# Third layer of a four-layer model: the recurrence woven, pair by pair, between units of its own later projections

## The reference, cut to what matters

```python
def hgrn2_mixer(h, w_in, lb, gate_norm_w, w_out):
    proj = h @ w_in
    q, f, i, g = jnp.split(proj, [HGRN_FDIM, 2 * HGRN_FDIM, 2 * HGRN_FDIM + D_MODEL], axis=-1)
    q = jax.nn.silu(q)
    log_f = jnp.logaddexp(jnp.log(lb), jnp.log1p(-lb) + jax.nn.log_sigmoid(f32))
    k = (1.0 - lb) * jax.nn.sigmoid(-f32)
    o = hgrn2_recurrence(q.reshape(shp), k.reshape(shp), log_f.reshape(shp), i.reshape(...))
    o = rms_norm(o, gate_norm_w) * jax.nn.silu(g.reshape(...))
    return o.reshape(B, S, D_MODEL).astype(h.dtype) @ w_out
```

## Time and profile before

| | |
|---|---|
| median of 3 runs | 2283.85 us (2283.8 to 2285.46) |
| profiled execution | 2282.78 us |
| its span, first to last instruction | 2280.8 us |
| PE busy, share of the span | 2151.5 us, 94% |
| VectorE busy | 1072.6 us, 47% |
| ScalarE busy | 823.5 us, 36% |
| GpSimd busy | 225.3 us, 10% |
| mean granted clock of PE | 0.963 |

### The profile page before, as it was taken

How to read it: one execution, slowest core, us unless ns; L and a number is a source line. 1 busy time by engine, 2 the same in 40 slices (tenths; PEclk the granted TensorE clock), 3 DMA queues, 4 the chain that set the end, 5 groups by cost and what they waited for, 6 DMA issues and landing times. The chain is left out here.

```text
span 2280.8 us, 27066 instructions
## 1 busy us (share of the span) xinstructions
PE 2151.5 (94%) x10717; PEld 1772.2 (78%) x10717; DVE 1072.6 (47%) x1877; ACT 823.5 (36%) x1515; POOL 225.3 (10%) x347
## 2 busy tenths in 40 slices
PE   6999989999999999999897999999899979999998
PEld 5887557888887877878786888888778658888887
DVE  5343766565554345233984533433433555334333
ACT  3154754443333234322012422323432664223322
POOL 8200000100000001001542100000100011000000
PEclk9999999999999999999656999999999989999999
DMA  5435412233332222322000223322233103222321
GB/s 127 99 111 92 52 38 88 82 99 99 104 93 93 93 93 82 103 101 74 1 1 9 94 93 100 103 93 93 84 129 129 56 1 102 93 93 96 107 93 74
DMA packets 162107, 192.00 MB, mean 84 GB/s; under 512 B 22866, under 2 KB 133757, under 8 KB 161981
## 3 DMA queue, kind: packets, MB, share of 16 engines
q1 hardware_dynamic: 157536, 176.15, 24.4%
q0 software_dynamic: 3904, 13.97, 3.3%
q10 hardware_dynamic: 541, 0.15, 0.0%
HBM read 182.91 MB, written 7.34 MB: 83 GB/s over the span
## 5 line engine op out<-in xcount | busy, mean ns | idle before, releaser
L1396 DVE TENSOR_TENSOR WHL<-raw,WHL 128x1024 fp32r<-128x1024 f32 x312 | 385.6, 1237 | 700.3 <-ACT WHL L869 700.0
L869 ACT ACTIVATE WHL<-raw 128x1024 fp32r<-128x1024 f32 x312 | 328.5, 1054 | 570.3 <-PE bank L2247 395.6
L2247 PE MATMUL bank<-WHL,HXh 128*128 128x512 f32 x1632 | 442.7, 393 | 5.4 <-DVE HXl L1405 4.0
L2098 PE MATMUL bank<-HXh,WHL 128*128 128x512 f32 x1120 | 438.8, 392 | 4.1 <-ACT BIG L1026 1.6
L2100 PE MATMUL bank<-HXh,WHL 128*128 128x512 f32 x1120 | 436.6, 390 | 0.0
L2247 PEld LDWEIGHTS bank<-WHL,HXh 128*128 128x128 f32 x1632 | 308.4, 190 | 72.4 <-issue 7.2
L2099 PE MATMUL bank<-HXl,WHL 128*128 128x512 f32 x928 | 361.6, 390 | 0.0
L2247 PE MATMUL bank<-WHL,HXl 128*128 128x512 f32 x816 | 252.9, 391 | 0.0
L2098 PEld LDWEIGHTS bank<-HXh,WHL 128*128 128x128 f32 x1120 | 211.0, 188 | 49.4 <-issue 5.4
L2100 PEld LDWEIGHTS bank<-HXh,WHL 128*128 128x128 f32 x1120 | 210.7, 188 | 44.3
L2099 PEld LDWEIGHTS bank<-HXl,WHL 128*128 128x128 f32 x928 | 174.5, 188 | 35.5
(11 more groups left out here) (322 smaller groups left out, 3052.4 us busy)
## 6 DMA issues: line engine op xcount, KB each, us to landing
raw<-in_mlp_w_up_dram SPq DMA_DIRECT2D x64, 512.0 KB, 4.6
raw<-in_mlp_w_down_dram SPq DMA_DIRECT2D x64, 512.0 KB, 4.3
raw<-in_w_up_dram SPq DMA_DIRECT2D x44, 512.0 KB, 5.1
raw<-in_a_w_in_dram SPq DMA_DIRECT2D x32, 512.0 KB, 4.5
raw<-in_w_in_dram SPq DMA_DIRECT2D x24, 512.0 KB, 4.8
raw<-in_w_down_dram SPq DMA_DIRECT2D x22, 512.0 KB, 4.3
raw<-in_w_kv_dram SPq DMA_DIRECT2D x16, 512.0 KB, 4.5
rel_dram<-GB POOLq DMA_DIRECT2D x1, 5120.0 KB, 54.0
```

The source lines that it names most:

```text
L869: return a.activation(dst, src, ACT.Copy, **k)
L1396: v.tensor_tensor(dst(1), src, dst(0).bitcast(F32), ALU.subtract).then_inc(w_lo, 1)
L2098: m.matmul(b[:, :], w[0][:, k, :], x[0][:, k, :], start=(k == 0), stop=False)
L2247: ins = m.matmul(ybank(tt, h)[:, :], x, w[:, h * HALF:(h + 1) * HALF], start=(k == 0 and i == 0), stop=(k == nk - 1 and i == 2))
```

## The change

The weights of this layer are cut into eight blocks and used in a new order: qf0 (query and forget projections of heads 0 and 1), hi0, qf1, hg0, qf2, hi1, qf3, hg1, where hi and hg blocks are halves of 512 columns. qf0 is done in `norm_halves(3)`. The recurrence starts then: pair p has 8 steps, and step s holds the level product of the pair and, behind it in PE's stream, dense unit 8p + s, as long as there is one (28 in all; in the first step of a pair the level product stands in the middle of the unit). The level products of a pair share two banks (5 and 7), the dense units have four (4, 6, 0, 2), and states, keys, outputs and turns of the pair before use banks 1 and 3. VectorE and GpSimd treat a pair in one operation of twice the columns. The full decay is multiplied into hQ and hK in place, and the chunk states go into used parts of hF. The output product is cut by column half and feature block (`out_product`, 12 products): two pieces stand in steps 5 and 6 of the last pair, four between the last two heads' work, and ten follow. Its weights are loaded as blocks of 512 columns. The arithmetic is the same. The core of the diff (left out: renamed counters and most of the lines that the new loops replace, the bodies of the products, the masked copy of a pair, the per-head helpers that lose an argument, the new helpers of ScalarE, `projected`, `dense_out`, `out_high`, `keys_evac`, which evacuate one dense unit, then split the unit three ahead, round a feature block of the output, or copy the turned keys):

```diff
+DENSE = ("hi0", "qf1", "hg0", "qf2", "hi1", "qf3", "hg1")
...
+    for name in ("qf0",) + DENSE:
+        i = int(name[2:])
+        if name[:2] == "qf":
+            cols8(name, a_in, 256 * i, 256)
+            cols8(name, a_in, D + 256 * i, 256, at=1)
+        else:
+            blocks(name, a_in[:, (2 if name[:2] == "hi" else 3) * D:][:, 0:D], i)
+    blocks4("h_out", t["a_w_out_2"][0])
...
-          ("hq", 8, "act"), ("hf", 8, "act"), ("hi", 8, "vec"), ("hg", 8, "act"),
+          ("qf0", 4, "act"), ("hi0", 4, "vec"), ("qf1", 4, "act"), ("hg0", 4, "act"), ("qf2", 4, "act"),
+          ("hi1", 4, "vec"), ("qf3", 4, "act"), ("hg1", 4, "act"),
...
+        def state(h, c):
+            return hF[:, h, (384, 0, 128)[c]:(384, 0, 128)[c] + P]
+        def of_pair(x, p):
+            return x[:, 2 * p:2 * p + 2, :].rearrange("p h t -> p (h t)")
+        LV, DB = (bank[5], bank[7]), (bank[4], bank[6], bank[0], bank[2])
...
+            for p in range(HH // 2):
+                a, b = 2 * p - 2, 2 * p - 1
+                for l in range(1, NL):
+                    w = LEVELS[l]
+                    pool.wait_ge(s_grown, NL * p + l)
+                    pool.wait_ge(lv_psum, level_count(p, l if l > 1 else 0))
+                    g.tensor_tensor(halves_of(klv, w)[0], halves_of(of_pair(hK, p), w)[0], halves_of(sfx2, w)[0],
+                                    ALU.mult).then_inc(klv_ready, 1)
+                    if l == 4 and p:
+                        head_gain(a)
+                        head_gain(b)
+                        head_stats(a)
+                if p:
+                    head_stats(b)
+                pool.wait_ge(s_grown, NL * (p + 1))
+                g.tensor_tensor(of_pair(hK, p), of_pair(hK, p), sfx2, ALU.mult).then_inc(ks_ready, 1)
+                if p < HH // 2 - 1:
+                    pool.wait_ge(ks_ready, p + 1)
+                    g.memset(sfx2, 1.0).then_inc(s_set, 1)
...
+            for p in range(HH // 2):
+                a_, b_ = 2 * p - 2, 2 * p - 1
+                for s in range(NL + 1):
+                    if p and s == 1:
+                        if p > 1:
+                            head_evac(b_ - 2)
+                        keys_evac(a_)
+                    elif p and s == 2:
+                        keys_evac(b_)
+                    elif p and s == 4:
+                        head_out(a_)
+                    elif p and s == 6:
+                        head_evac(a_)
+                        head_out(b_)
+                    if 8 * p + s < 4 * len(DENSE):
+                        dense_out(8 * p + s)
+                    if p == HH // 2 - 1 and s == 3:
+                        for k in range(4):
+                            out_high(k)
+            w, a_, b_ = unit_at["h_out", 0], HH - 2, HH - 1
+            out_high(4)
+            split(w + 3)
+            head_evac(5)
+            keys_evac(a_)
+            out_high(5)
+            keys_evac(b_)
+            split(w + 4)
+            head_out(a_)
+            head_out(b_)
+            split(w + 5)
+            head_evac(a_)
+            out_high(6)
+            head_evac(b_)
+            out_high(7)
+            split(w + 7)
+            split(unit_at["up0", 0] + 1)
...
+            def level_ops(p, l):
+                w = LEVELS[l]
+                ends = [2 * T // (2 * w), w]
+                f1, f2 = halves_of(of_pair(hF, p), w)
+                if l:
+                    vec.wait_ge(lv_psum, level_count(p, l))
+                    vec.wait_ge(vec_chain, grown[0])
...
                 else:
+                    vec.wait_ge(ps_free["act"], GT[f"qf{p}"][2] + 4)
+                    if p:
+                        vec.wait_ge(lv_psum, level_count(p - 1, NL))
+                v.tensor_tensor(qlv.rearrange("p (b w) -> p b w", w=w), halves_of(of_pair(hQ, p), w)[1], f2,
+                                ALU.mult).then_inc(lv_ready, 1)
+                if l:
+                    masked(p, l)
+                vec.wait_ge(*((klv_ready, (NL - 1) * p + l) if l else (s_set, p + 1)))
+                s1 = halves_of(sfx2, w)[0]
+                v.tensor_tensor(s1, s1, f2[:, :, w - 1:w].to_broadcast([P] + ends), ALU.mult).then_inc(s_grown, 1)
+                vec.wait_ge(s_grown, NL * p + l + 1)
+                vec.wait_ge(lv_ready, NL * p + l + 1)
+                chain(v.tensor_tensor(f2, f2, f1[:, :, w - 1:w].to_broadcast([P] + ends), ALU.mult))
+                grown[0] = chain.n
+                if not l:
+                    masked(p, 0)
...
+            for p in range(HH // 2):
+                a_, b_ = 2 * p - 2, 2 * p - 1
+                for s in range(NL + 1):
+                    if s < NL:
+                        level_ops(p, s)
+                    else:
+                        vec.wait_ge(vec_chain, grown[0])
+                        v.tensor_tensor(of_pair(hQ, p), of_pair(hQ, p), of_pair(hF, p), ALU.mult).then_inc(hs_ready, 1)
+                        masked(p, NL)
+                    if p and s in (2, 3):
+                        states(a_ + s - 2)
+                    elif p and s == 5:
+                        gated_h(a_)
+                    elif p and s == NL:
+                        gated_h(b_)
+                    if 8 * p + s < 4 * len(DENSE):
+                        split(w0 + 8 * p + s + 2)
+                    if s == 3 and p in (0, 2):
+                        for tt in range(TT):
+                            vec.wait_ge(ps_full, GT[f"hi{p // 2}"][0] + tt + 1)
+                            v.tensor_copy(hI[:, tt, HALF * (p // 2):HALF * (p // 2 + 1)],
+                                          DB[tt][:, :]).then_inc(ps_free["vec"], 1)
+                    if p == HH // 2 - 1 and s in (4, 5):
+                        out_low(2 * s - 8)
+                        out_low(2 * s - 7)
+            w, a_, b_ = unit_at["h_out", 0], HH - 2, HH - 1
+            split(w + 2)
+            out_low(4)
+            states(a_)
+            out_low(5)
+            states(b_)
+            split(w + 3)
+            gated_h(a_)
+            split(w + 4)
+            gated_h(b_)
+            out_low(6)
+            out_low(7)
+            split(w + 7)
+            split(unit_at["up0", 0] + 1)
...
+            def level_product(p, s):
+                if p or s:
+                    pe.wait_ge(lv_masked, level_count(p - 1, NL) if s == 0 else level_count(p, max(s - 2, 0)))
+                if s == 0:
+                    pe.wait_ge(ps_free["act"], GT[f"qf{p}"][2] + 4)
+                else:
+                    pe.wait_ge(lv_ready, NL * p + s)
+                if s > 1:
+                    pe.wait_ge(klv_ready, (NL - 1) * p + s - 1)
...
+            def dense(c, middle=None):
+                block, u = divmod(c, 4)
+                name = DENSE[block]
+                if name[:2] == "qf":
+                    w = [y.rearrange("p (k c) -> p k c", k=KD) for y in unit(name, u)]
+                    bank_wait(block, u)
+                    for k in range(KD):
+                        ins = feature_product(DB[u], w, (HXh, HXl), k)
+                    ins.then_inc(ps_full, 1)
+                    return
+                wh, wl = (y.rearrange("p (k c) -> p k c", k=2) for y in unit(name, u))
+                for tt in range(TT):
+                    if u == 0:
+                        bank_wait(block, tt)
+                    if tt == 2 and middle is not None:
+                        level_product(*middle)
...
+            def out_product(k, tts=range(TT)):
+                half, j, u = k // KD, k % 2, k // 2
+                wh, wl = (y.rearrange("p (k c) -> p k c", k=2)[:, j, :] for y in unit("h_out", u))
+                k %= KD
+                if half == 0:
+                    pe.wait_ge(x_lo, x0["h_out"] + k + 1)
+                for tt in tts:
+                    if half == k == 0:
+                        bank_wait(len(DENSE), tt)
...
+            for p in range(HH // 2):
+                a, b = 2 * p - 2, 2 * p - 1
+                for s in range(NL + 1):
+                    c = 8 * p + s
+                    if s == 0:
+                        dense(c, (p, 0))
+                        continue
+                    level_product(p, s)
+                    if p and s == 1:
+                        if p > 1:
+                            head_turn(b - 2)
+                        keys_turned(a)
+                    elif p and s == 2:
+                        chunk_states(a)
+                        keys_turned(b)
+                    elif p and s == 3:
+                        chunk_states(b)
+                    elif p and s == 4:
+                        outputs(a)
+                    elif p and s == 6:
+                        head_turn(a)
+                        outputs(b)
+                    if c < 4 * len(DENSE):
+                        dense(c)
+                    elif s == 5:
+                        out_product(0)
+                    elif s == 6:
+                        out_product(1)
             a, b = HH - 2, HH - 1
```

(49 more changed lines are left out.)

410 lines of the change are left out of this document (157 added, 253 removed).

## The result

The changed kernel takes 2202.61 us (median of 4 runs, 2194.37 to 2203.93) against 2283.82 beside it: a ratio of 0.9645, 95% interval 0.9629 to 0.9661. Forecast were 2205. Run once more later it took 2200.39 (0.9639, 0.9625 to 0.9653).

What follows compares the result with a forecast made beforehand. Bound taken: a serial recurrence chain, VectorE first, on a lower-clocked PE. Terms 156.8 + 85.2 + 43.8 + 2.2 + 3.5 + 5 + 2 = 298.5 us against 377.0, giving 2205; range 2196 to 2236 with two rivals.

Steps and rivals of the forecast that it cites:

- item 8: Granted PE clock: 0.63 in the old recurrence becomes 1.00; 2 us for lower-clock records in the last pair's thin steps.
- Item 1: PE's stream, same work interleaved: dense 156.8 us with 3.6 of stalls, 728 records at 0.117 (85.2), output products 43.8.
- Item 2: PE switching between level and dense products: 35 places at 0.1 us, 3.5 us; bounds none and 10 us.
- Item 3: VectorE handling two heads per operation: 3.6 us a level and pair instead of 4.5, hidden behind PE.
- Item 4: GpSimd's key product at 512 columns: 1.33 to 1.41 us, with 5.47 us available; 18 us at most of 66 a pair.
- contention rival: VectorE and GpSimd in each other's way in the recurrence: 12 us more in four pairs, 2217; chance 0.12.
- Items 5 and 6: ScalarE evacuations, some 7 table loads of 1.28 us, hidden; weight loads reordered, same bytes, splits with 7.3 us to spare.
- Item 7: Last pair and tail, where cover is thin: 5 us of PE idle time together; bounds none and 12.7 us.
- Outside the stretch: Beyond projections, recurrence and output product (377.0 us together), the change was said to touch nothing.
- A falling clock in the thin steps: Rival: lower PE clock for the last pair's thin steps and the tail, 31 us more, 2236; chance 0.10.
- Half clock throughout: Rival: all 28 mixed steps get only the lower clock, 273 us more, 2478; chance 0.04.
- nothing hidden: Rival: splits and dense units wait, each step's costs stay apart, no change at 2284; chance 0.02.

Runs made afterwards that it cites:

- 1: Changed kernel with all 28 dense units ahead of the recurrence, not interleaved, pair-wide operations and output pieces kept: 2278.58 us (ratio 0.999).
- 2: As 1, plus eight unused dense products on PE behind each of the first 24 level products: 2261.42 us (0.9908).
- 4: Changed kernel with each 512-column pair operation on VectorE and GpSimd split into two of 256, one per head: 2196.14 us (0.9627).
- 5: Changed kernel plus two unused VectorE products of 384 columns in each of the 28 steps: 2199.36 us (0.9634).
- 6: Changed kernel plus six unused VectorE products of 384 columns in each of the 28 steps: 2233.95 us (0.9788).
- 3: Changed kernel with the six early output pieces moved behind the last head, out of the last pair and tail: 2216.43 us (0.9712).
- 9: Changed kernel plus three unused two-input GpSimd products of 384 columns behind each key product: 2204.38 us (0.9659).
- 7: Changed kernel with GpSimd's memsets held back until the norm's scaling is over: 2193.44 us (0.9618), a second time 2195.23 (0.9616).

## Why the prediction was right

- **The reading of the bottleneck.** Right, and shown by 1 and 2: taking only the interleaving away gives 2278.58, and unused products give 21.6 us back. The gain is PE's clock and its waits. Fewer instructions on VectorE or GpSimd are no part of it (4). One reading was loose: the 0.7 and 1.6 us of item 8 are idle time of the weight loads; PE's own before the same products were 0.49 and 1.51.
- **Item 1, the order of PE.** Right in kind, too dear in two terms. The first 28 units should have taken 153.2 of dense products, 3.6 of stalls, 590 records x 0.117 = 69.0, and about 2.8 for switches, 228.6 us; from 918.46 on they took 218.9. The stalls of the old dense part are not in the new one, and 218.9 less 153.2 and 2.8 leaves 62.9 for 590 records: 0.107 each. The 0.117 was a merged row's length divided by its count; it holds the overhang of the last record. From start to start, a step of 7.27 less 24 x 0.228 and the switch leaves 1.7 us for 16. This is nearly the sum's whole error within the stretch: of the 10.5 us between 298.5 and 288.0, 3.6 are stalls and 6.1 the price of these records.
- **Item 2, switches.** Right: 934.70 to 935.02 is 0.32 us for the first dense product behind a level product, instead of 0.23, so 0.09 against the forecast's 0.1.
- **Item 3, VectorE by pairs.** Forecast 3.6 us a level, measured 3.2, with means of 0.69 to 0.89, below the 1.1 that would have refuted it. Hidden, with about 80 us to spare in 28 steps (5, 6).
- **Item 4, GpSimd.** A key product takes 1.67, not 1.33 to 1.41. It matters nowhere but in the last pair. That wider operations wait for each other was in the contention rival, not in this term.
- **Items 5 and 6.** Right: seven table loads of 1.28, no wait of PE for ScalarE before the tail, none for a load; the loads went on at 69 GB/s where they had stopped.
- **Item 7, the last pair and the tail.** Forecast 5 us of idle time, measured 4.6, but otherwise spread: 2.03 before the first output product where 0.8 was put, since GpSimd's two gains stretched two of VectorE's operations to 1.74 and 1.63; 1.51 for one gated head; the waits put at the last two heads' other hand-overs were covered. 3 shows what the weaving of the tail is worth, 14 to 16 us.
- **Item 8, the clock.** Right: 1.00 in the 28 steps, 0.96 in the thin ones, some 3 us at the half clock, which cost 1.5 (2 forecast). The first output product already starts at full clock. What the clock does when PE has pauses of 2 us in each step of the first pair is kernel 1, and that it is the pauses is kernel 2.
- **Outside the stretch.** "Outside them the change touches nothing" was the step that failed. The change made two memsets of 512 columns beside the norm's scaling into four of 1024 and lost 3.9 us there: 2.6 of longer waiting (4.08 instead of 1.45), and about 1.3 at the half clock behind it, where products of 256 columns start 0.21 apart from 902.93 to 905.71 instead of 0.12. Another 4.6 us are within the spread that unchanged code shows from profile to profile. The two errors, 10.5 too much inside and 8.5 too little outside, nearly cancel: the profiled span is 80.5 less, forecast were 78.5. That the total came within 3 us is luck; the mechanism and most of its terms are not.

**The rivals.** Contention of VectorE and GpSimd: real for single operations, but with a price of only 1.1 us on PE in the covered steps when GpSimd is given 85 us more (9). The Trainium skill, GPSIMD Engine Reference, Specifications, names VectorE instructions with two SBUF inputs as those that contend, and beside them those in a 2-port mode; the prediction took only the first. The norm's scaling, with one tensor input, was held up by memsets (7). The Trainium skill, SBUF — State Buffer, Who interferes with whom, says that such scalings can enter a mode that uses the port pair shared with GpSimd, and that whoever issues first has it for the whole instruction. That the scaling was in that mode no run shows, and on the order the trace does not bear the sentence out: by the records the scaling started at 896.65, 0.52 us ahead of the first memset, and still ended behind the last. The prediction had looked for contention only inside the recurrence. A falling clock in the thin steps: about 1.5 of the 31 us that it was priced at; the Trainium skill, TensorE: Matmul & The Clock Gate, A second HAM failure mode, describes a loop whose small holes make the clock swing, and kernel 1 behaves so (16 records in 3.65 us at 1128.02, in 1.90 at 1134.11), the changed one does not. Half clock throughout, and nothing hidden: excluded by the clock of 1.00 and the 7.27 us of a step.

## What to carry to other kernels

A serial chain of small products costs PE twice, once in waits and once in the clock, so the best filler is dense work that must be done anyway, even if the helper engines do not get faster. Wider operations on the helpers save nothing by themselves and may give up an overlap between heads; look at them together with the cover. Price pipelined records from start to start, never from a merged row's length, and give the filler step more time than the slowest helper (here 7.3 us against VectorE's 4.8). When a change reshapes buffers, look also at the set-up operations that it widens: a memset on GpSimd can stand in VectorE's way, at a moment when PE waits for VectorE.

## What the runs showed of the hardware that had not been expected

Where an operation of VectorE with two inputs from SBUF starts while a product of GpSimd of 384 columns or more runs, it ends a fixed time behind GpSimd's instruction: 0.54 to 0.56 us for 512 columns (0.69 us alone) and 1.08 to 1.09 us for 1024 (1.22 alone), in the changed kernel and in kernel 9. So it does nearly all of its work after GpSimd has ended: a split from 967.24 took 3.42 us beside GpSimd's product of 1024 columns, which ended at 969.58. Rows of both engines in the changed kernel:

```profile
1139.41 2.94 POOL L806 TENSOR_TENSOR GM<-GM,subg 128x512 f32<-128x512 f32 x2
1139.48 1.74 DVE L1954 TENSOR_TENSOR PB<-PB,BIG 128x512 f32<-128x512 f32 x1 [0.53 <-POOL PB L816]
...
1141.26 1.63 DVE L1957 TENSOR_TENSOR BIG<-BIG 128x512 f32<-128x512 f32 x1
```

The two gains take 1.263 and 1.705 us. The first ends at 1140.67, VectorE's suffix at 1141.22; the second ends at 1142.35, VectorE's decays at 1142.89. So the two take turns by whole instructions, and the second gain was held up in its turn. The scaling had no such turn among the memsets: the last of four ended at 900.82 and the scaling at 901.37, 0.55 later, so 0.75 us of work took 4.72. In the kernel before, the two memsets ended at 896.60 and the scaling at 897.15, again 0.55 later. Memsets do not hold up everything: in kernel 7 a split, with two inputs, took its 1.22 us from 893.49 while the memsets ran from 893.70, although it too had started just before them. Why gains let VectorE in between and memsets do not stays open; the memsets' rows overlap (0.97 long, 0.89 apart). The masked copy, whose data come from PSUM, took its 0.70 us beside a running key product in the changed kernel (at 1130.27, the key product from 1129.77 to 1131.49).

The second surprise is how far unchanged code moves: 877.2 to 882.2 us up to the same turn. A gain of 5 us could be called one only from the part of the span that the change owns, together with a control run beside it.
